# A six-slot expert ring with four held chunks of w_q, and a lead-in with an earlier w_out and a one-unit-ahead mLSTM gate

## The reference, cut to what matters

```
h  = modulate(rmsnorm(x));  z = h @ w_in
x += gate1 * W_out[ mLSTM heads (forward and backward) || windowed attention heads ]
x += gate2 * peer(modulate(rmsnorm(x)))

peer: q = x @ w_q                  # 1024 x 2048, 8 heads of two 128-wide halves
      top 16 of 128 keys on either side, top 16 of the 256 sums -> 8*16 = 128 experts a token
      a = gelu(x . u_tab[expert]);  out = sum(gate * a * v_tab[expert])
```

## Time and profile before

| what | value |
|---|---|
| median of three runs | 3620.82 us |
| the profiled execution's own time | 3620.1 us |
| its span, first to last instruction | 3618.3 us |
| TensorE busy | 72% |
| VectorE busy | 68% |
| ScalarE busy | 27% |
| GpSimd busy | 40% |
| gathered by the software queue | 1208.03 MB, 80.0% of the 16 DMA engines' span |
| other DMA (queue 1) | 138.75 MB, 10.5% |
| mean DMA rate over the span | 378 GB/s |
| mean granted TensorE clock | 0.863 |

### The profile page before, as it was taken

How to read it: one execution, slowest core, us unless ns; L and a number is a source line. 1 busy time by engine, 2 the same in 40 slices (tenths; PEclk the granted TensorE clock), 3 DMA queues, 4 the chain that set the end, 5 groups by cost and what they waited for, 6 DMA issues and landing times.

```text
span 3618.3 us, 30605 instructions
## 1 busy us (share of the span) xinstructions
PE 2607.5 (72%) x9522; PEld 1002.0 (28%) x9522; DVE 2452.2 (68%) x5535; ACT 988.5 (27%) x2690; POOL 1463.4 (40%) x1297
## 2 busy tenths in 40 slices
PE   8999787878878888676576566557656755775555
PEld 3455465333323333221121112112111211221111
DVE  3665547876786768558767768676776768676655
ACT  1232333433434244312222122122212211221111
POOL 0110134444544345444444444444434444444443
PEclk9999998899989899797798789779977977987777
DMA  8222577999999999999999999999999999999999
GB/s 304 101 101 89 192 250 291 407 401 414 413 426 425 424 394 420 401 425 415 427 427 427 427 421 427 418 416 427 413 427 423 427 421 419 427 418 427 410 427 381
DMA packets 226295, 1368.59 MB, mean 378 GB/s; under 512 B 25402, under 2 KB 36290, under 8 KB 77650
## 3 DMA queue, kind: packets, MB, share of 16 engines
q0 software_dynamic: 165888, 1208.03, 80.0%
q1 hardware_dynamic: 53040, 138.75, 10.5%
q10 hardware_dynamic: 7204, 19.85, 1.4%
HBM read 1338.02 MB, written 28.52 MB: 378 GB/s over the span
## 4 chain that ended last, share of the span: by engine, by line
DMA 41%; PE 31%; DVE 14%; POOL 5%; issue 4%; ACT 4%; SPq 1%; ACTq 0%; POOLq 0%; DVEq 0%
DMA fx_ring<-arg_uv,fx_eidx 38%; PE fx_acc L1675 12%; PE in_z L587 10%; DVE fx_ring L2137 8%; POOL fx_ring L1375 4%; PE at_sP L1523 3%; ACT fx_weighted_pick L1830 2%; DVE rt_rest L2010 1%; DVE rt_ab L2012 1%; PE rt_qP L1548 1%; DVE rt_rest L2008 1%; PE at_aP L1459 1%; DMA rt_w_q<-arg_w_q 1%; ACT fx_gelu L1826 1%; PE at_sP L1548 1%
## 5 line engine op out<-in xcount | busy, mean ns | idle before, releaser
L1675 PE MATMUL fx_acc<-fx_ring,fx_weighted_pick 128*64 128x512 f32 x4608 | 1437.0, 756 | 911.0 <-ACT fx_weighted_pick L1830 890.3
L1375 POOL DMA_INDIRECT fx_ring<-arg_uv,fx_eidx x1152 | 1325.4, 1150 | 1639.7 <-PE fx_acc L1675 1446.4
L2137 DVE CUSTOM_DVE_ANT_0 fx_ring<-fx_ring,fx_h 128x1024 f32<-128x1024 f32 x1152 | 1406.0, 1232 | 762.8 <-DMA fx_ring<-arg_uv,fx_eidx 758.1
L1675 PEld LDWEIGHTS fx_acc<-fx_ring,fx_weighted_pick 128*64 128x64 f32 x4608 | 330.9, 160 | 1893.4 <-ACT fx_weighted_pick L1830 1359.1
L1826 ACT ACTIVATE fx_gelu<-fx_dot 128x2 f32<-128x2 f32 x576 | 117.1, 203 | 2105.5 <-DVE fx_dot L2137 2104.7
L1830 ACT ACTIVATE fx_weighted_pick<-fx_weighted_pick,fx_gelu 128x64 f32<-128x64 f32 x1152 | 338.0, 340 | 54.5 <-ACT fx_gelu L1826 1.5
L1548 PE MATMUL rt_qP<-rt_w_q,rt_h2T 128*128 128x512 f32 x384 | 193.9, 630 | 11.4 <-DMA rt_w_q<-arg_w_q 11.4
L587 PE MATMUL in_z<-w_in,in_hT 128*128 128x512 f32 (+1 forms) x480 | 197.9, 569 | 2.8 <-DMA w_in<-arg_w_in 2.8
L587 PE MATMUL in_z<-w_in,ml_gate_sums 128*128 128x512 f32 (+1 forms) x384 | 154.0, 559 | 0.0
L1523 PE MATMUL at_sP<-at_w_out,at_mixT 128*128 128x512 f32 x288 | 136.8, 620 | 3.7 <-DVE at_mixT L1903 3.7
L527 POOL COPY in_turned<-in_heads 128x320 f32<-128x320 f32 x9 | 9.1, 1009 | 320.9 <-DVE in_heads L758 320.9
(11 more groups left out here) (359 smaller groups left out, 2463.4 us busy)
## 6 DMA issues: line engine op xcount, KB each, us to landing
rt_wq<-arg_w_q SPq DMA_DIRECT2D x40, 512.0 KB, 7.8
fx_ring<-arg_uv,fx_eidx POOLq DMA_INDIRECT x1152, 12.7
ml_qkT<-arg_w_ada SPq DMA_DIRECT2D x22, 512.0 KB, 4.5
ml_qkT<-qkT_scratch SPq DMA_DIRECT2D x18, 512.0 KB, 7.2
ada_w<-arg_w_ada SPq DMA_DIRECT2D x8, 1024.0 KB, 13.5
w_in<-arg_w_in SPq DMA_DIRECT2D x32, 256.0 KB, 7.1
rt_w_q<-arg_w_q SPq DMA_DIRECT2D x16, 512.0 KB, 32.7
ml_kv<-kv_scratch SPq DMA_DIRECT2D x14, 514.0 KB, 6.2
```

The source lines that it names most:

```text
L1375: pool.indirect_dma_start(out=ring[j][:], out_offset=None, in_=io.uv, in_offset=bass.IndirectOffsetOnAxis(ap=eidx[t % 2][:, i:i + 1], axis=0),
L1675: mm = pe.matmul(acc[b][cg * TOKS:(cg + 1) * TOKS, :], wsel[:, i % (2 * FILL), :], ring[i % GROUP][:, D + b * 512:D + (b + 1) * 512], star ...
L2137: dve.tensor_tensor_reduce(out=ring[j][:, 0:D], in0=ring[j][:, 0:D], in1=h2r[t % 2][cg][:], scale=1.0, scalar=0.0, op0=ALU.mult, op1=ALU.a ...
```

## The change

Five things, in one diff.

1. `GROUP` becomes 6, so `DEPTH` is 3 pairs, and a slot is chosen by the gather's number over all tiles, since 128 is no multiple of 6. The wait of the selection matrices' refill stays four pairs back.
2. The 16 KB a partition that two slots took hold four chunks of `w_q` (3, 7, 11, 15): loaded once in pair 4 of tile 0, used by the routing of tiles 1 to 8, and left out of the streams of tiles 1 and 2 and of the resident load.
3. `w_out` is loaded in `project_in`, into the columns of `w_in` that hold C_Q and C_K, once TensorE is through with them in the last tile.
4. In the mLSTM, TensorE transposes the gate columns of unit u+1 right behind the scores of unit u, and ScalarE makes unit u+1's exponentials behind unit u's scaling; the gate sums are loaded two steps earlier. The last two units no longer weight keys nor update the state, which nothing reads.
5. Tile 0's x1 is stored, and two w_q chunks and gate1 are loaded, in step 4 of `route(0)` in place of step 14 of the mixer.

```diff
-GROUP = 8
+GROUP = 6
...
     for k in range(KD):
-        sp.dma_start(g.w_in[:, k, c0:c1], io.w_in[k * P:(k + 1) * P, c0:c1]).then_inc(g.s_w_in[i], 16)
+        sp.dma_start(w_in_columns(g, k, c0, c1), io.w_in[k * P:(k + 1) * P, c0:c1]).then_inc(g.s_w_in[i], 16)
...
+                sp.wait_ge(s_z, (TILES - 1) * 6 + 4)
+                for k in range(KD):
+                    sp.dma_start(g.w_out[:, k, :], io.w_out[k * P:(k + 1) * P, :]).then_inc(g.s_wo, 16)
...
-    GROUP = 8
     DEPTH = GROUP // NC
...
+    HELD = (3, 7, 11, 15)
...
-        return m % WQ
+        if m % NSIDE in HELD:
+            return None
+        return sum(i % NSIDE not in HELD for i in range(NSIDE, m)) % WQ
...
+        held = [sb(f"rt_w_q_held{i}", [P, HALF]) for i in range(len(HELD))]
...
+                        if k == 4 and t == 0:
+                            store_x1(0)
+                            chunk(HQ + 2)
+                            chunk(HQ + 3)
...
-                            for k in range(KD):
-                                sp.dma_start(w_out[:, k, :], io.w_out[k * P:(k + 1) * P, :]).then_inc(s_wo, 16)
...
+                    if t == 0 and r == 4:
+                        for i, m in enumerate(HELD):
+                            k, half = m % KD, m // KD
+                            sp.dma_start(held[i][:], io.w_q[k * P:(k + 1) * P, half * HALF:(half + 1) * HALF]).then_inc(s_held, 16)
...
+                                if half * KD + k in HELD:
+                                    continue
                                 sp.dma_start(w_q[:, k, part], io.w_q[k * P:(k + 1) * P, part]).then_inc(s_wqr[half], 16)
...
-                        j = i % GROUP
+                        j = (t * SLOTS + i) % GROUP
...
+                def columns(u):
+                    t, d = divmod(u, 2)
+                    pe.wait_ge(s_r, u - 1)
+                    if u >= 3:
+                        pe.wait_ge(s_cols, u - 2)
...
+                    gate_columns(pe, g, misc, d, tiles(t)[d], u < FIRST).then_inc(s_col, 1)
...
                         mm.then_inc(s_qk, 1)
+                        if 1 <= u < UNITS - 1:
+                            columns(u + 1)
...
+                        if 1 <= u < UNITS - 1:
+                            exponentials(u + 1)
...
-                        dve.wait_ge(s_cd, u * 2 + (p + 1))
-                        for j in range(2):
+                        if u < UNITS - 2:
+                            dve.wait_ge(s_cd, u * 2 + (p + 1))
+                        for j in range(2 if u < UNITS - 2 else 0):
...
-                        if n > DEPTH:
-                            dve.wait_ge(s_acc, n - DEPTH)
+                        if n > FILL // NC:
+                            dve.wait_ge(s_acc, n - FILL // NC)
```

More of the change, by code:

```diff
@@ L65, with w_in_columns @@
 CELL = MW + MH * C1
+def w_in_columns(g, k, c0, c1):
+    if c1 <= C_V:
+        return g.w_out[:, k, c0:c1]
+    return g.w_in[:, k, c0 - C_V:c1 - C_V]
 def load_w_in(sp, g, io, i):
@@ L1025, in mix_and_experts @@
         gex = sb("rt_gexp", [P, PH, TOPK])
-        with ExitStack() as early:
+        w_out = g.w_out
+        with g.early as early:
             def esb(name, shape, dt=F32):
@@ L1208, in mixer, with store_x1 @@
                             load_head(t + 1)
[L1209 to L1215, removed]
+                        if k == 14 and t:
+                            store_x1(t)
                         yield
+                def store_x1(t):
+                    sp.wait_ge(s_x1, t * 2 + 2)
+                    sp.dma_start(g.x1_dram[t], x1[:]).then_inc(s_x1o, 16)
                 def chunk(m):
-                    if m < NSIDE * STREAMED:
+                    if m < NSIDE * STREAMED and buffer_of(m) is not None:
                         if before(m) is not None:
@@ L1250, in begin @@
                 def begin():
+                    sp.wait_ge(s_hd, UNITS)
                     for d in range(2):
@@ L1534, in query @@
                         m = t * NSIDE + half * KD + k
-                        if t < STREAMED:
+                        if t and m % NSIDE in HELD:
+                            pe.wait_ge(s_held, 16 * len(HELD))
+                            w = held[HELD.index(m % NSIDE)]
+                        elif t < STREAMED:
                             i = buffer_of(m)
@@ L1603, in route @@
                         yield
+                def columns(u):
[3 more added lines that the diff above has]
+                        pe.wait_ge(s_cols, u - 2)
+                    if u == FIRST:
+                        pe.matmul(misc[:, 2 * P:2 * P + 2 * MH * TILES], g.ones[:],
+                                  ends[:].rearrange("p r h t -> p (r h t)"), start=True, stop=True)
+                    gate_columns(pe, g, misc, d, tiles(t)[d], u < FIRST).then_inc(s_col, 1)
                 def mlstm():
@@ L1650, in mlstm @@
                                 pe.wait_ge(s_t, u * 2 - 2)
-                            for j in range(2):
-                                h = 2 * p + j
-                                mm = pe.matmul(R[2 - p][:, j, 0:C1], kk[i][:, h, :], v1[i][:, h, :], start=True, stop=True)
-                            mm.then_inc(s_cd, 1)
+                            if u < UNITS - 2:
+                                for j in range(2):
+                                    h = 2 * p + j
+                                    mm = pe.matmul(R[2 - p][:, j, 0:C1], kk[i][:, h, :], v1[i][:, h, :], start=True, stop=True)
+                                mm.then_inc(s_cd, 1)
                             if p == 0:
@@ L1781, in store_h, with exponentials @@
                     act.dma_start(g.h_dram[d, tiles(t)[d]], hd[d]).then_inc(s_hst[d], 16)
+                def exponentials(u):
+                    d = u % 2
+                    act.wait_ge(s_col, u - 1)
+                    act.wait_ge(s_den, u - 1)
+                    if u >= 4:
+                        act.wait_ge(s_gk, u - 3)
+                    last = gate_exponentials(act, g, misc, d, u < FIRST)
+                    if u == FIRST:
+                        last = act.activation(decay[:].rearrange("p r h t -> p (r h t)"),
+                                              misc[:, 2 * P:2 * P + 2 * MH * TILES], ACT.Exp)
+                    last.then_inc(s_cols, 1)
+                    act.wait_ge(s_cols, u - 1)
+                    act.wait_ge(s_eb[d], ADA_LOADS + u // 2 * 16 + 16)
+                    act.wait_ge(s_o, u * 2 - 2)
+                    decays(act, g, d).then_inc(s_e, 1)
                 def mlstm():
```

58 lines of the change are left out of this document (21 added, 37 removed).

## The result

The changed kernel takes 3821.07 us, the median of 4 runs (3819.19 to 3825.7). The kernel before took 3623.1 us beside it, in 4 runs (3619.7 to 3625.63). The ratio is 1.0552, with a 95% interval from 1.0539 to 1.0564: 5.5% slower. The forecast was 3667 us and slower, with a range up to 3735. The direction was right, the size was not: the loss is 198 us and not 47.

What follows compares the result with a forecast made beforehand. The prediction took the DMA engines' gathers as the bound, 427 GB/s or 4.91 us a pair. Lead-in -25, held chunks -8 and ring +80 gave +47 on 3620: 3667 us, range 3608 to 3735.

Steps and rivals of the forecast that it cites:

- The bound: Whole gather stage: DMA engines limit it at 427 GB/s, 4.91 us a pair, with about four gathers always queued.
- Part 1, the ring: Six slots in place of eight: cover for delays shrinks by 4.91 us, costing +80 us, from +34 to +144.
- I take 6.5 us for a gather that finds little ahead of it: Landing time assumed for a six-slot refill, leaving 2.5 us of room on the fast TensorE clock, 1.0 on the slow.
- The 9 and 11 dips: Stretches under 405 GB/s: 9 in tiles 3 to 8 to cost 26 us more, 11 in tiles 0 to 2, 54.
- Rival (c): Six slots leave no cover in every slow pair: ring +145, sum +112, 3732 us; tile 4 over 332 us; chance 0.17.
- the second rival: Six slots are deep enough: ring costs 10 to 34 us, total 3597 with the middle at 3608; chance 0.15.
- Part 2, the held chunks: w_q loads in tiles 1 and 2: 4.2 MB less to move, -8 us, between 2 and 20 saved.
- Parts 3 to 5, the lead-in: Work before the first gather shortens by 25 us, between 10 and 38; first fetch at about 568 us.
- The term for `w_out`: Lead-in: loading w_out in the last projection tile lets VectorE's part of the head norm start sooner, -10 us.
- the term for the x1 store: Lead-in: SyncE's wait for x1 no longer precedes the gate sums, so about 6 of 12.3 us go.
- taking a gate's exponentials out of the chain can gain only what TensorE idles, about 10 us, and I take 5: Lead-in, from the scaling of x1 to the end of the products: 5 us saved.
- rival (d): Lead-in bound by TensorE: -10 in place of -25, the rest as forecast, 3682 us; chance 0.06.

Runs made afterwards that it cites:

- the two put-back runs: New lead-in with eight slots and no held chunks; one returns the w_out loads, the other the x1 store, chunks and gate1, to their old places: 3611.34 and 3612.58 us.
- the dummies: Changed kernel plus three unread 512-column products behind every pair of tile 8 and pairs 0 to 12 and 51 to 63 of tiles 3 to 7: 3742.89 us.

## Why the size was wrong, step by step

**The bound.** Right for eight slots: 427 GB/s, 4.91 us a pair, and the ring always full. In the changed kernel the bound is another one, the cycle of a slot.

**Part 1, the ring: forecast +80, measured +213 in the stage and +219 alone.** The failed step is this sentence: "I take 6.5 us for a gather that finds little ahead of it", and with it "A calm stretch still fits, so the ring costs nothing there". The row it came from had the answer: the second gather of the stage landed in 8.44 us with one ahead of it. The prediction took 2.46 us off for the one ahead, and went for a value between the least of all 1152, 5.7 us, and its own reading of the first, 7.5. But in this kernel gathers are issued two by two, so the one that completes a pair always has one ahead of it; with nothing else in the queue it still takes 7.6 us. With 8.44 in place of 6.5 the prediction's own sum leaves 14.7 - 5.7 - 8.44 = 0.6 us of room on the fast clock and -1.0 us on the slow one, and no calm stretch fits.

What the traces show, put as the first gather of a refill, which is issued 4.16 + 0.28 = 4.44 us after the pair's last landing (5.89 + 0.28 = 6.17 with a slow clock). To keep the transfers back to back in a ring of G slots it must land G - 1 transfers of 2.456 us after that landing. Room is that less the way; beside it the median from issue to landing, over pairs 200 to 569:

| slots | room, fast | landed | room, slow | landed |
|---|---|---|---|---|
| 8 | 17.19 - 4.44 = 12.75 | 12.73 | 11.02 | 11.24 |
| 6 | 12.28 - 4.44 = 7.84 | 8.50 | 6.11 | 7.89 |

With eight slots the gathers land just when their turn comes. With six and a slow clock they land 1.8 us after it. The second gather of the refill, which completes the pair, shows why. It is issued 5.7 us after the landing (7.4 with a slow clock), and its turn comes after six transfers, so it has 9.0 us, or 7.3. The run with one pair ahead has 7.6 us for it with nothing in the queue but its partner. With a slow clock no pair can fit, then; with a fast one it does, by 1.4 us. Measured, it landed after 9.5 us (fast) and 9.0 us (slow); with eight slots it has 14.0 and 12.3 us and lands after 13.9 and 12.3. Why it is 9.0 us and not nearer to 7.6 is not shown. In tile 8 with a fast clock throughout, the rate nearly returns. With seven slots the gather that completes a pair is the first to be issued after a release, and has 14.74 - 4.44 = 10.30 us, or 8.57; it landed after 10.2 in tiles 3 to 7, in the median. That is a whole transfer more than six, not the 1.2 us of the expectation, and even 8.57 is over the 7.9 us that such a gather took with six slots and a slow clock: tiles 3 to 8 lose nothing. By these rows, an estimate, the edge lies between 6.1 and 8.6 us of room for the first gather.

The other half of the failed step is the TensorE clock. The prediction weighed it by the granted clock (0.83 to 0.91) and wrote that most pairs are fast. That is so: of the 384 pairs of tiles 3 to 8, 143 were slow before and 182 after. But the slow ones carry the loss. The time from the landing of one pair to that of the next, in the mean, by the clock of the pair whose end released the refill:

| | released by a slow pair | by a fast pair |
|---|---|---|
| tiles 3 to 8, eight slots | 5.02 us | 5.02 us |
| tiles 3 to 8, six slots | 5.77 us | 5.10 us |
| tiles 0 to 2, eight slots | 5.59 us | 5.66 us |
| tiles 0 to 2, six slots | 6.54 us | 5.74 us |

In tiles 3 to 8 that is 0.75 us for each slow pair, some 136 us of the 154, and 0.08 us for each fast one.

The 9 and 11 dips that the prediction counted were not the loss. Stretches of 10 us under 405 GB/s went from 41 of 300 to 206 of 320; the forecast said "more than 80". Rival (c) named the mechanism that came, "the cover is gone in every slow pair", but priced it at 145, with half a microsecond in half of 576 pairs, and had it at 0.17; the slow pairs were fewer, 232 of 576, and cost more each, 0.75 us in tiles 3 to 8 and 0.95 in tiles 0 to 2. Tile 4 took 346 us, over the 332 which the prediction had as (c)'s mark.

The prediction cited the Trainium skill ("DMA: Bandwidth & Descriptors", Anatomy of one DMA) for an estimated 4.4 us of one transfer of 1 MB, and said that by that rule the second rival would be the outcome. The run with one pair ahead has 5.56 us for a gather in an empty queue, and 7.6 us for the one behind it, so 4.4 us is too low by a fifth for the first of two such gathers and by more for the second, and the outcome went the other way.

**Part 2, the held chunks: forecast -8, read -6.** The bytes are as worked out: 4.19 MB less on queue 1, all of it. The idle time of 11.4 us is gone, as the page's parts 3 and 5 have it (queue, packets, MB, share; group, busy us, mean ns, idle us); it did not show in the total, since with six slots and nothing held it was down to 2.3 us already, and to 1.0 with the new lead-in.

```profile
q1 hardware_dynamic: 51888, 134.56, 9.8%
...
L1573 PE MATMUL rt_qP<-rt_w_q,rt_h2T 128*128 128x512 f32 x288 | 148.5, 640 | 0.0
```

**Parts 3 to 5, the lead-in: forecast -25, measured -7.** The first gather was to be issued at 568 us and went at 586.80; over 585 was the mark for wrong. The chain of waits after, against the earlier trace rows:

```profile
452.36 5.16 PE at_sP L1545 x8
...
481.48 1.16 ACT rt_scores L1770
...
515.88 7.64 DMA ml_gate_sums<-gate_cum_scratch
...
586.80 1.15 POOL fx_ring L1397
```

Up to the scaling of x1 the trace has -9.4 us (490.89 before), though the projection ended 3 us later in it; -16 was forecast, 10 of them for `w_out` and 6 for the x1 store. Counted from the projection's end the two put-back runs say how it divides: the scaling starts after 75.7 to 78.6 us in the five old traces, 62.8 to 66.5 in the ten new ones, 73.3 with the late `w_out` and 66.2 with the late x1 store. The term for `w_out` holds, about 8 us of 10; the term for the x1 store was not found, and the 2 to 5 us left are of the other edits, which no run takes apart. From the scaling on, where 7 us more were forecast, nothing came: it is 102.6 us to the first gather before and 105.3 after. The term that "taking a gate's exponentials out of the chain can gain only what TensorE idles, about 10 us, and I take 5" fails, and part of what was won is given back. A gate sum's transfer is on the chain again, 7.64 us from 515.88. SyncE's timeline (start us, us, operation) has what stood ahead of its issue:

```profile
508.35 6.22 SPq L1236 DMA_DIRECT2D rt_wq<-arg_w_q  x2
...
515.88 0.43 SPq L291 DMA_DIRECT2D ml_gate_sums<-gate_cum_scratch  x1
```

Two chunk loads, which wait for the query products that free their buffers, hold SyncE for 6.2 us, and the sums of a unit are now needed one unit sooner. The wait for gate sums was not removed but moved. The product of the mix does start 7 us sooner (452.36, 459.43 before), and from there to the first gather TensorE has 90 of the 134 us of the chain. That comes near the prediction's rival (d), -10, at its 0.06.

**What stays open.** In tiles 0 to 2 six slots cost 60 us, and the dummies were not tried there. The table above says that the slow pairs carry most of it, 47 pairs of 0.95 us, and seven slots give two thirds of the 60 back; but it sorts pairs as they came, and no run changed the clock there. In the middle of tiles 3 to 7, 53 slow pairs remained with the dummies; sorted in the same way (6.07 us against 5.02 with eight slots) they hold about three quarters of the last 74 us (2001.2 against 1927.3). That is a sorting too, and VectorE's steps are not told apart from it.

## What to carry to other kernels

Take the transfer whose landing the loop waits for (here the second of two), and count the transfers at the full rate from a slot's landing to its turn. A ring's depth can be enough only when these, less the time from the landing to its issue, are over the time that it takes to land with nothing else queued but what the loop always issues with it: 7.6 us here, against 7.3 with six slots and a slow clock, and 12.3 with eight. Take that time from a row in which the gathers stand as the loop will issue them, and take nothing off. Do the sum for the slowest common state of the engines on the way (here the low TensorE clock, in 143 of 384 pairs), since with no room left every such pair counts. A kernel can sit one buffer from the edge and show nothing of it: eight slots to seven cost 22 us, seven to six 195.

## What the runs showed that was not expected

- Products that nobody reads raised the granted TensorE clock of tile 8 from 0.72 to 0.99 and took 30 us off it, with six slots. Where TensorE had 4.9 us a pair and 1.9 us of work, three products of 512 columns went unnoticed; where the routing's products stood as well, they cost 25 us a tile.
- Products into the two 64-column halves of TensorE run side by side, and both counts come at the end (0.06 us apart in all 576 pairs), so an order by slot releases nothing earlier.
- A gather of 128 rows of 8 KB takes 5.56 us from issue to landing in an empty queue, and one issued 1.24 us behind it 7.6 us (medians over 576 pairs).

The fastest version that ran is the new lead-in with eight slots: 3613.07 us (0.9964 to 0.9995 of before), or 3611.69 with the dummy products in the quiet stretches (0.9961 to 0.9984). The two are not told apart.
